# Latent attention's keys prepared by pairs of heads, rotated rows once a layer, row minima as softmax biases

## The reference

```python
q = (rms_norm(c_q, q_norm_g) @ w_uq).reshape(b, t, 8, 96)
kv = (rms_norm(c_kv, kv_norm_g) @ w_ukv).reshape(b, t, 8, 64 + 64)
k = concatenate([broadcast(k_rope), kv[..., :64]], -1)      # 32 rotary rows are the same for all heads
q = apply_partial_rope(rms_norm(q, q_head_g), cos, sin)
k = apply_partial_rope(rms_norm(k, k_head_g), cos, sin)
p = softmax(q @ k^T * 96**-0.5)                             # per head; differential attention: 64**-0.5
```

## Time and profile before

| | us |
|---|---|
| median of 3 runs (lowest, highest) | 2167.85 (2161.13, 2168.57) |
| profiled execution | 2165.82 |
| its span, first to last instruction | 2164.0 |
| PE busy | 2022.3 |
| DVE busy | 1085.6 |
| POOL busy | 1001.9 |
| ACT busy | 830.9 |

### The profile page before, as it was taken

How to read it: one execution, slowest core, us unless ns; L and a number is a source line. 1 busy time by engine, 2 the same in 40 slices (tenths; PEclk the granted TensorE clock), 3 DMA queues, 4 the chain that set the end, 5 groups by cost and what they waited for, 6 DMA issues and landing times.

```text
span 2164.0 us, 32558 instructions
## 1 busy us (share of the span) xinstructions
PE 2022.3 (93%) x13234; PEld 1754.1 (81%) x13234; DVE 1085.6 (50%) x1721; ACT 830.9 (38%) x1364; POOL 1001.9 (46%) x593
## 2 busy tenths in 40 slices
PE   7999998889789999999999999988888899999999
PEld 7988987567668999999999889885565577888887
DVE  7533377666765544441037332676656765444300
ACT  4322343677563222222234222444666623222211
POOL 4365444774323444444434455337853234444443
PEclk9999999999999999999999999999999999999999
DMA  4211112000002222223322111111000022323333
GB/s 167 70 59 60 60 49 69 10 1 30 21 20 60 89 95 90 88 89 98 98 87 79 59 59 59 51 58 40 1 20 30 20 81 94 95 91 97 98 102 112
DMA packets 40325, 143.80 MB, mean 66 GB/s; under 512 B 4592, under 2 KB 4976, under 8 KB 40048
## 3 DMA queue, kind: packets, MB, share of 16 engines
q1 hardware_dynamic: 40176, 141.72, 20.6%
HBM read 139.60 MB, written 2.10 MB: 65 GB/s over the span
## 4 chain that ended last, share of the span: by engine, by line
PE 75%; DVE 12%; ACT 7%; issue 5%; POOL 1%; DMA 0%; SPq 0%; DVEq 0%; ACTq 0%; POOLq 0%
PE pb L873 35%; PE pb L908 7%; PE pb L909 7%; PE pb L910 7%; PE pb L946 4%; PE pb L948 3%; PE pb L947 3%; DVE rowmax L2004 2%; PE pb L1331 2%; PE pb L1323 1%; ACT rstd L1480 1%; ACT ebuf L1515 1%; PE pb L1032 1%; ACT proj_r L1536 1%; POOL parts L651 1%
## 5 line engine op out<-in xcount | busy, mean ns | idle before, releaser
L651 POOL TENSOR_TENSOR parts<-raw,parts 128x1024 fp32r<-128x1024 f32 x248 | 606.8, 2447 | 791.8 <-ACT parts L1574 791.7
L1574 ACT ACTIVATE parts<-raw 128x1024 fp32r<-128x1024 f32 x248 | 262.5, 1059 | 834.5 <-PE pb L873 405.4
L873 PE MATMUL pb<-proj_r,parts 128*128 128x264 f32 x3104 | 427.5, 285 | 0.5 <-POOL parts L651 0.5
L873 PEld LDWEIGHTS pb<-proj_r,parts 128*128 128x128 f32 x3104 | 399.3, 189 | 0.8 <-issue 0.7
L873 PE MATMUL pb<-mix,parts 128*128 128x264 f32 x2208 | 333.7, 293 | 22.1 <-DVE mix L1906 13.1
L873 PEld LDWEIGHTS pb<-mix,parts 128*128 128x128 f32 x2208 | 299.3, 195 | 26.7 <-DVE mix L1906 13.5
L946 PE MATMUL pb<-mix,parts 128*128 128x264 f32 x800 | 242.9, 304 | 1.3 <-DVE proj L1939 1.3
L948 PE MATMUL pb<-mix,parts 128*128 128x264 f32 x800 | 229.8, 287 | 0.0
L947 PE MATMUL pb<-mix,parts 128*128 128x264 f32 x800 | 229.5, 287 | 0.0
L908 PE MATMUL pb<-proj_r,parts 128*128 128x512 f32 x528 | 207.5, 393 | 0.8 <-DVE mbuf L1930 0.8
L910 PE MATMUL pb<-proj_r,parts 128*128 128x512 f32 x528 | 207.7, 393 | 0.0
(11 more groups left out here) (290 smaller groups left out, 3288.8 us busy)
## 6 DMA issues: line engine op xcount, KB each, us to landing
raw<-w_stream SPq DMA_DIRECT2D x250, 512.0 KB, 3.5
w_head<-w_heads SPq DMA_DIRECT2D x8, 512.0 KB, 4.0
h<-x_t SPq DMA_DIRECT2D x8, 264.0 KB, 4.7
out_t<-h SPq DMA_DIRECT2D x8, 256.0 KB, 4.8
con<-consts SPq DMA_DIRECT2D x1, 1652.5 KB, 9.9
par<-params SPq DMA_DIRECT2D x1, 170.0 KB, 6.8
par<-params SPq DMA_DIRECT2D x1, 166.0 KB, 6.1
con<-consts SPq DMA_DIRECT2D x1, 128.0 KB, 6.6
```

What stands on the lines that cost most here:

```text
L651: nc.gpsimd.tensor_tensor(parts[:, n % PARTS, 1, :], w, parts[:, n % PARTS, 0, :].bitcast(FP32), ALU.subtract).then_inc(split.sem, 1)
L873: last = nc.tensor.matmul(pb[rows_, 2 * p + a, 0:HALF], lhs_t, rhs[:, a * HALF:(a + 1) * HALF], start=start, stop=stop)
L1574: nc.scalar.activation(parts[:, n % PARTS, 0, :], raw[:, r % RAW, :], ACT.Copy).then_inc(lead_ready.sem, 1)
```

## The change

1. Keys by pairs of heads. One product gives the 64 unrotated rows of two heads, on 128 partitions, into the tile KK; there are 4 such preparations a layer, 12 in all. Their squares are summed per half by the table `ones_h`. The weights' columns are put in the order of the pairs by four loads instead of one. DVE writes the two heads' keys with one instruction each.
2. Rotated rows once a layer. The squares of the 48 rotary rows are summed once (`rope_sum`) and POOL adds them to each pair's squares (`key_square`). The rows themselves get gain and rotation once a layer, in piece 61 of the input tiles (`rope_turn`), and POOL multiplies them by each head's root (`key_rows`).
3. The scale and a minus sign stand in the gains of the queries (`gain_q`); the scores are negative, a reduction by minimum gives the exponential's bias, and the exponential has scale -1.

```diff
-PREPS = [(0, 0), (0, 1), (1, 0), (1, 1)] + [(hd, side) for hd in range(2, MLA_H) for side in (1, 0)]
+PREPS = [(0, 0), (0, 1), (1, 0)] + [e for m in range(1, MLA_H // 2) for e in ((m, 1), (2 * m, 0), (2 * m + 1, 0))]
+KK, RSTD_K, ROPE_SUM = MQ, MQ + 1, MK
+               + [(57, "rope_square", 0)] + [(61, "rope", 0)]
-        OPENING = (("p", 0, 0), ("p", 1, 0), ("t", 0, 0), ("p", 3, 0), ("t", 1, 0), ("p", 2, 0), ("v", 3, 0), ("t", 2, 0), ("p", 4, 0),
-                   ("p", 0, 1), ("p", 1, 1), ("t", 3, 0), ("t", 4, 0), ("v", 4, 0), ("p", 2, 1), ("p", 3, 1), ("v", 0, 0), ("v", 1, 0),
-                   ("p", 4, 1), ("v", 2, 0))
+        OPENING = (("r", 0, 0), ("p", 0, 0), ("p", 1, 0), ("t", 0, 0), ("p", 3, 0), ("t", 1, 0), ("p", 2, 0), ("v", 3, 0), ("t", 2, 0),
+                   ("p", 4, 0), ("p", 0, 1), ("p", 1, 1), ("t", 3, 0), ("t", 4, 0), ("v", 4, 0), ("p", 2, 1), ("v", 0, 0), ("v", 1, 0),
+                   ("v", 2, 0))
@@ prepare
-                    prep(stage, hd + 2)
+                    if stage < 3:
+                        prep(stage, hd + 2)
+                    elif hd % 2 == 0:
+                        prep(stage, hd // 2 + 1)
@@ SP
+            for l in range(DEPTH):
+                sp.dma_start(gain_k[MLA_NOPE:2 * MLA_NOPE, l, :], params[0:MLA_NOPE, l, a:a + 2]).then_inc(par_in.sem, 16)
+                        to = w_head[:, 0, :].rearrange("p (m b a n) -> p m a b n", b=2, a=2, n=MLA_NOPE)
+                        src = w_heads[4 * l, :, :].rearrange("p (m a b n) -> p m a b n", a=2, b=2, n=MLA_NOPE)
+                        for a in range(2):
+                            for b in range(2):
+                                sp.dma_start(to[:, :, a, b, :], src[:, :, a, b, :]).then_inc(head_in[0].sem, 16)
@@ POOL
+            def key_square(l, e):
+                s = SQ_M + e
+                pool.wait_ge(rope_summed.sem, rope_summed.at(l, 1))
+                pool.wait_ge(sq_ready.sem, sq_ready.at(l, s + 1))
+                nc.gpsimd.tensor_tensor(sq[:, s % 2, :], sq[:, s % 2, :], tile_of(proj, ROPE_SUM), ALU.add).then_inc(k_added.sem, 1)
+                pool.wait_ge(k_added.sem, k_added.at(l, PREPS[e][0] + 1))
+            def key_rows(l, e):
+                m, low, both = PREPS[e][0], slice(0, 48), slice(MLA_NOPE, MLA_ROWS)
+                pool.wait_ge(rs_ready.sem, rs_ready.at(l, RS_M + e + 1))
+                pool.wait_ge(rope_low.sem, rope_low.at(l, 1))
+                pool.wait_ge(s_ps.sem, s_ps.at(l, max(2 * m - 1, 0) * n_q(l)))
+                link(nc.gpsimd.tensor_tensor(k_head(2 * m)[both, :], tile_of(proj, MISC, rows_=low), tile_of(proj, RSTD_K, rows_=low), ALU.mult))
+                nc.gpsimd.tensor_tensor(k_head(2 * m + 1)[both, :], tile_of(proj, MISC, rows_=both), tile_of(proj, RSTD_K, rows_=both),
+                                        ALU.mult).then_inc(roped.sem, 1)
+            def rope_turn(l):
...
+                link(nc.gpsimd.memset(turned[64:96, :], 0.0))
+                link(nc.gpsimd.tensor_scalar(own[both, :], own[both, :], par_at(l, "kh_g", rows_=both), None, ALU.mult))
...
+                nc.gpsimd.tensor_tensor(own[both, :], own[both, :], turned[both, :], ALU.add).then_inc(rope_turned.sem, 1)
-                for e in range(2 * MLA_H):
+                for e, (n, side) in enumerate(PREPS):
+                    if side:
+                        key_square(l, e)
+                        key_rows(l, e)
+                        continue
...
+                    if n in (2, 4):
+                        for k in range(2 * n - 4, 2 * n):
+                            mixed_split(l, k)
@@ PE
+                def rope_sum():
+                    pe.wait_ge(rope_squared.sem, rope_squared.at(l, 1))
+                    product(1, C("ones", slice(0, 48)), tile_of(proj, MISC, rows_=slice(0, 48)), True, True).then_inc(rope_ps.sem, 1)
...
+                            o = (2 * n + c) * P
+                            last = product(p, w_head[:, 0, o:o + P], tile_of(proj, CKV + c), c == 0, c == 1)
...
+                        if side:
+                            pe.wait_ge(k_added.sem, k_added.at(l, n + 1))
+                        norm_sum(l, SQ_M + e, 1, p, rws, "ones_h" if side else "ones")
@@ ACT
-                nc.scalar.activation(halves(to[:, b, :]), pair(b), ACT.Exp, scale=scale_of(l, n), bias=negmax[:, b:b + 1],
+                nc.scalar.activation(halves(to[:, b, :]), pair(b), ACT.Exp, scale=-1.0, bias=negmax[:, b:b + 1],
+                def rope_sum():
+                    act.wait_ge(rope_ps.sem, rope_ps.at(l, 1))
+                    nc.scalar.activation(halves(tile_of(proj, ROPE_SUM)), pair(1), ACT.Copy, scale=1.0 / MLA_NOPE).then_inc(rope_summed.sem, 1)
@@ DVE
-                link(nc.vector.tensor_reduce(rowmax[:, n % 2:n % 2 + 1], pair(n % 2), AX.XY, ALU.max))
-                nc.vector.tensor_scalar(negmax[:, n % 2:n % 2 + 1], rowmax[:, n % 2:n % 2 + 1], -scale_of(l, n), None,
-                                        ALU.mult).then_inc(max_ready.sem, 1)
+                nc.vector.tensor_reduce(negmax[:, n % 2:n % 2 + 1], pair(n % 2), AX.XY, ALU.min).then_inc(max_ready.sem, 1)
+                        link(nc.vector.tensor_scalar(gain_q[:, 0:1], par_at(l, "qh_g"), -MLA_QK ** -0.5, None, ALU.mult))
+                        link(nc.vector.tensor_scalar(gain_q[:, 1:2], par_at(l, "dq_g"), -DIFF_QK ** -0.5, None, ALU.mult))
-                        if side == 1:
-                            nc.vector.tensor_copy(buf[kr, :], tile_of(proj, MISC, rows_=kr))
+                    elif stage == 3:
+                        dve.wait_ge(p_ps.sem, p_ps.at(l, e + 1))
+                        nc.vector.tensor_copy(halves(tile_of(proj, KK)), pair(prep_pair(n, side))).then_inc(p_copy.sem, 1)
+                    elif stage == 4:
+                        dve.wait_ge(s_ps.sem, s_ps.at(l, max(2 * n - 1, 0) * n_q(l)))
+                        dve.wait_ge(rs_ready.sem, rs_ready.at(l, RS_M + e + 1))
+                        high = slice(MLA_NOPE, 2 * MLA_NOPE)
+                        for rows_, gain, dst in ((nope, par_at(l, "kh_g", rows_=nope), k_head(2 * n)),
+                                                 (high, gain_k[high, l, 0:1], k_head(2 * n + 1))):
+                            last = nc.vector.scalar_tensor_tensor(out=dst[nope, :], in0=tile_of(proj, KK, rows_=rows_), scalar=gain,
+                                                                  in1=tile_of(proj, RSTD_K, rows_=rows_), op0=ALU.mult, op1=ALU.mult)
+                        last.then_inc(rs_used.sem, 1)
```

More of the change, by code:

```diff
@@ L109 @@
 SQ_M = sum(n for _, _, n in NORMS)
[L110 removed]
+N_PREP = MLA_H + MLA_H // 2
+SQ_A = SQ_M + N_PREP
 SQ_O = SQ_A + 4
@@ L354, in query_sums @@
             return pb[rows_, 6, 0:SEQ] if layer == DEPTH - 1 else pair(3, rows_)
-        def scale_of(layer, n):
-            return MLA_QK ** -0.5 if n < n_att_m(layer) else DIFF_QK ** -0.5
         def turn_unit(layer, u):
@@ L424, in trunk, with prep_pair, opening @@
         OUT_BANK = (4, 5, 5, 4, 5)
-        def prep_pair(hd, side):
-            return ((0, 1), (3, 1))[hd][side] if hd < 2 else 3
-        def opening(value, turned_out, prep):
-            for what, k, hd in OPENING:
+        def prep_pair(n, side):
+            return side if n == 0 else 3
+        def opening(value, turned_out, prep, rope_sum):
+            for what, k, n in OPENING:
                 if what == "p":
-                    prep(k, hd)
+                    prep(k, n)
+                elif what == "r":
+                    rope_sum()
                 elif what == "t":
@@ L662, in rotate @@
             def rotate(l, e):
-                hd, side = PREPS[e]
-                buf, half = k_head(hd) if side else qh[:, hd % 2, 0:T], MLA_ROPE // 2
+                hd, half = PREPS[e][0], MLA_ROPE // 2
+                buf = qh[:, hd % 2, 0:T]
                 first, second, both = slice(64, 64 + half), slice(96, 96 + half), slice(MLA_NOPE, MLA_ROWS)
@@ new lines, in rope_turn @@
+            def rope_turn(l):
+                half = MLA_ROPE // 2
+                first, second, both = slice(64, 64 + half), slice(96, 96 + half), slice(MLA_NOPE, MLA_ROWS)
+                own, turned = tile_of(proj, MISC), qh[:, 0, 0:T]
+                pool.wait_ge(split.sem, split.at(l, G_SSD + 61 // PIECES + 2))
+                pool.wait_ge(o_ready.sem, o_ready.at(l, 1))
+                pool.wait_ge(rope_squared.sem, rope_squared.at(l, 1))
+                pool.wait_ge(c_ps.sem, c_ps.at(l, N_STATE))
+                link(nc.gpsimd.memset(turned[64:96, :], 0.0))
+                link(nc.gpsimd.tensor_scalar(own[both, :], own[both, :], par_at(l, "kh_g", rows_=both), None, ALU.mult))
+                link(nc.gpsimd.tensor_tensor(turned[second, :], own[first, :], C("sin_m", first), ALU.mult))
+                link(nc.gpsimd.tensor_tensor(turned[first, :], own[second, :], C("sin_m", second), ALU.mult))
```

(14 more changed lines are left out.)

109 lines of the change are left out of this document (65 added, 44 removed).

## The result

The changed kernel takes 2185.31 us (median of 4 runs, 2181.93 to 2188.62) against 2166.46 for the kernel before: ratio 1.0092, 95% interval 1.0074 to 1.0109. I had forecast 2171, range 2158 to 2182. It is slower than before by more than the 0.5% bound, and outside my range. The profiled execution took 2188.62, 3.3 us over that median, and its span is 2186.8, so the trace shows +22.8 us of span where the medians show +18.9.

A forecast was written before the change was run, and what follows sets the result against it. PE, busy for 93% of the span, was taken to bound the kernel. The terms 13.4 + 7.5 - 6.5 + 7.6 - 8.3 - 9.2 + 1.0 = +5.5 on 2165.82 gave 2171 us, range 2158 to 2182.

The forecast's parts named there:

- Opening, +13.4: Latent attention's opening: the key sum waits for POOL, 8.9 - 3.1 + 0.9 = +6.7 us a layer, +13.4 in all.
- the second rival: Openings cost their whole delay, PE returning at lower clock: +10.6 us each instead of +6.7, total 2179; chance 0.22.
- That rival's other half: In the opening the second query's product, not DVE's norm pair, comes last; part of the rival with chance 0.22.
- Pair blocks, +7.5 and +7.6: Loop blocks of heads 0, 2, 4: waits for POOL's addition and slower DVE norms, +7.5 us layer 0, +7.6 layer 1.
- Blocks without key work, -6.5 and -8.3: Loop blocks of heads 1, 3, 5 lose their key part: net -6.5 us in layer 0, -8.3 in layer 1.
- The note on the four splits: Heads 1 and 3: POOL's four splits in a row slow DVE's query norm, +0.8 us in four blocks.
- Row minima, -9.2: Multiplication after each reduction goes: -6.5 us in differential attention, -2.7 in latent attention, together -9.2.
- The rest, +1.0: Rotary rows' turning, taken to hide (1.5 uncovered), small DVE gains and tiny loads: +1.0 us, bounds 0 and +4.
- The key weights' four loads, 0: First key weights in four loads with 256-byte runs, issued some 8 us early: 0, upper end 2 us a layer.
- "slower": Whole kernel over 2179 us: half the second rival, half the third, a tenth of the forecast; chance 0.24.
- the openings' upper bound: Both openings, if removed work was covered by waits anyway: +9.8 us a layer; entered in the range as +6.4.

The follow-up runs named there:

- e16: The changed kernel with useless PE work filling the opening's waits: seven products before the wait for POOL's addition, six matmuls before the value product; 2185.7 us.
- e6: e2's kernel with POOL's two multiplications of rotated key rows waiting until DVE's two key norms are done; 2153.3 us, ratio 0.9947.
- e10: e6's kernel with the eight splits spread two by two behind the rotations of queries 2 to 5; 2171.8 us.
- e1: The kernel before with the row minima, scale and sign in the queries' gains alone, nothing of the keys; 2153.7 us, ratio 0.9944.
- e2: The changed kernel with POOL adding the first key pair's rotary squares before it rotates the first query; 2164.7 us, ratio 0.9992.
- e8: e2's kernel without the once-a-layer gain and rotation of the keys' rotary rows, one tiny memset in their place; 2165.3 us.
- e14: The changed kernel with gain_q's two small instructions behind column_copies instead of ahead of an evacuation; 2182.6 us.
- e9: e5 and e6 together, on e2's kernel: PE adds the rotary sum, and POOL's key rows wait for DVE's norms; 2146.6 us, ratio 0.9912.
- e11: The kernel before with eight extra useless matmuls a layer before three norm sums of the input stage; 2159.7 us, ratio 0.9978.
- e5: e2's kernel with PE adding the rotary squares' sum by an identity product, POOL's addition and PE's wait for it removed; 2166.5 us.

## Why the prediction was wrong, step by step

The step that failed is the half clock: the sum has it at nothing, and only one rival gave it 1.7 us for each opening. The runs show it behind added waits in the input stages, the openings and the loops: +25.5 us of loss, +19.9 where PE works, and 5.2 us of time in the openings alone. Beside it DVE's norm pair was put too short, and so was the turning of the rows. The trace is 17.3 us over the sum: 4.8 in the openings, 7.5 in the loops, 7.3 in start, input and dense stages, less 2.4 in differential attention.

- **Opening, +13.4: measured +18.2.** The walk of the stall was right. Stall, place and length are as put down (7 to 8 us forecast, 7.15 seen; the key sum is 8.3 late, 8.9 walked), and the delay without the clock's part is 2 x 6.5 = 13.0 (e16). What failed is that I left the half clock to the second rival and priced its clock at 1.7 us; it is 2.6 in each opening of these traces. That rival's other half, that the product and not DVE is last, was not so: DVE's norms and the gate held PE for another 2.69 us. The norm pair took 3.61, not 2.8.
- **Pair blocks, +7.5 and +7.6: measured +12.9 and +8.6.** PE's wait for the addition is 1.55 in layer 0 (1.4 walked) and 1.85 to 2.05 in layer 1. In layer 0, 5.3 us of the 12.9 are half-clock loss in heads 0 and 4; in layer 1, 3.4 of the 8.6. The root is the norm pair beside POOL (e6), which makes the last tile's turn wait 1.87.
- **Blocks without key work, -6.5 and -8.3: measured -6.8 and -9.3.** Right, to the handover cycle of 2.24 us (2.2 walked). The note on the four splits was right in kind: a wait of 2.14 us stands there once, in layer 0. That they are best left alone while POOL adds was not foreseen (e10).
- **Row minima, -9.2.** Right in place, a little small (work -10.4 in e1, median -12.8).
- **The rest, +1.0: measured +8.3 over start, input and dense stages.** This step was furthest off. 6.8 of the 8.3 is half-clock loss, of which part is chance: e2's trace, with the same code up to the opening, reaches it 4.9 us earlier (363.7 for 368.6). What is sure is the turning of the rows, priced at 1.5 at most and taken for hidden, which costs 2.3 us in layer 0 by way of DVE (e8), and the clock behind `gain_q`'s two instructions. Their own 0.38 us a layer were in the sum (0.4), but they stand ahead of an evacuation for which PE already waits, and with the clock they are some 1.3 us a layer, an estimate (e14).
- **The key weights' four loads, 0.** Right for the time: PE does not wait for them. A load of 128 KB with runs of 256 bytes takes 3.7 us, as long as one of 512 KB with long runs (3.7). The Trainium skill (DMA: Bandwidth & Descriptors, Specifications) asks for 512 bytes or more for the full rate; a quarter of the bytes in the same time neither shows that nor speaks against it, as no load of this size with long runs stands beside it.
- **Chances.** I gave the half clock one case of 0.22 and one place. It is not a mishap of one stall but a term of every wait added, so it belonged into the sum: +25.5 us over the span, of which not all is on the path (10.2 in the openings cost 5.2). Two slips besides: half, half and a tenth of the chances named make 0.205 for "slower", not 0.24, and the openings' upper bound is +6.2, not +6.4.

Undone by experiment, the loss reads: keys' part over the minima alone +31.6 (2185.3 - 2153.7); -20.6 by POOL's order in the opening (e2), -11.4 by DVE and POOL apart (e6), -6.7 by PE adding (e9), in all -38.7, so the pairs' own worth is some -7 before e11's and e14's steps.

## What to carry to other kernels

Before PE is made to wait for an in-order helper engine, list what stands ahead of that helper's instruction; if it is a rotation, give PE the addition as an accumulating product instead (e9: 6.7 us under e6; alone, in e5, it won nothing). Put a price on idle time of PE that includes the clock behind it, above all next to waits that are already there: 0.38 us more cost some 1.3, an estimate. But take the clock from many traces, not from one pair. DVE and POOL released by one event on the same memory hold each other up (DVE's pair 3.61 us instead of 1.53), so chain the one that nobody waits for behind the other; that alone was worth 11.4 us.

## What was not expected of the hardware

The loss by half clock differs between executions of the same kernel (mean clock 0.979 to 0.987 over e2's twelve runs), also in stretches that no edit touched (start of the kernel: 0, 1.7 or 3.4 us in different traces), so medians of 4 to 12 runs leave some 2 us open. Useless matmuls in three waits made the kernel before 0.22% faster. DVE's norm on 64 rows takes 0.76 us alone and 1.89 beside POOL, within 0.02 us in all eight places. Two DVE instructions on four columns took 2.04 and 1.24 us beside long ones of POOL, and 0.59 and 0.16 in e8.
